# Three weight chunks loaded and split in halves at the start, first products by block over three chunks

## What is computed

```python
def rms_norm(x, g):
    xf = x.astype(jnp.float32)
    y = xf * lax.rsqrt(jnp.mean(xf * xf, axis=-1, keepdims=True) + EPS)
    return (y * g.astype(jnp.float32)).astype(x.dtype)
...
    for l in range(DEPTH):
        h = rms_norm(x, norm_mix_pre[l])
        proj = h @ w_in[l]
        qa, ka, va, qb, kb, vb = jnp.split(proj, SPLITS, axis=-1)
```

## Time and profile before

| what | value |
|---|---|
| median of 3 runs | 1076.66 us (1076.03 to 1077.01) |
| the profiled execution | 1076.21 us |
| its span | 1074.3 us |
| TensorE, matmul | 1060.6 us busy, 99% of the span |
| TensorE, weight load | 937.0 us, 87% |
| VectorE | 883.5 us, 82% |
| ScalarE | 666.4 us, 62% |
| GpSimd | 187.9 us, 17% |
| granted TensorE clock | 1.00 |

### The profile page before, as it was taken

The page is one execution under the profiler, slowest core; times in us unless marked ns, Lnnn a source line. Parts: engine busy times, 40 slices in busy tenths (PEclk is TensorE's granted clock), DMA queues, the critical chain, the costliest instruction groups (busy, mean ns, idle before and its releaser), DMA issues.

```text
span 1074.3 us, 17989 instructions
## 1 busy us (share of the span) xinstructions
PE 1060.6 (99%) x6544; PEld 937.0 (87%) x6544; DVE 883.5 (82%) x1440; ACT 666.4 (62%) x1171; POOL 187.9 (17%) x239
## 2 busy tenths in 40 slices
PE   9999999999999999999999999999999999999997
PEld 6788777998999999988888787788899999998886
DVE  6898896799988988898685788766589889879876
ACT  7887785476555555666683469645455555566664
POOL 1576754011100111000000104210011111110000
PEclk9999999999999999999999999999999999999999
DMA  7423322766776676886636720154366676777553
GB/s 297 128 60 92 86 60 75 227 129 184 203 184 205 162 184 200 192 258 205 189 133 215 171 75 1 50 157 149 97 157 167 219 169 183 204 182 224 192 178 129
DMA packets 51319, 171.16 MB, mean 159 GB/s; under 512 B 6432, under 2 KB 7072, under 8 KB 51104
## 3 DMA queue, kind: packets, MB, share of 16 engines
q1 hardware_dynamic: 37296, 122.56, 34.9%
q0 software_dynamic: 13312, 46.14, 19.8%
q10 hardware_dynamic: 624, 1.31, 0.4%
HBM read 162.64 MB, written 48.23 MB: 196 GB/s over the span
## 4 chain that ended last, share of the span: by engine, by line
PE 89%; DVE 4%; ACT 3%; POOL 2%; issue 1%; DMA 1%; SPq 0%; DVEq 0%; ACTq 0%; POOLq 0%
PE bank L2214 11%; PE bank L2213 11%; PE bank L2212 11%; PE bank L2773 7%; PE bank L2774 7%; PE bank L2775 7%; PE bank L641 6%; PE bank L642 6%; PE bank L643 6%; PE bank L1245 2%; PE bank L1235 2%; PE bank L1190 1%; PE bank L1192 1%; PE bank L1191 1%; PE bank L1334 1%
## 5 line engine op out<-in xcount | busy, mean ns | idle before, releaser
L563 DVE TENSOR_TENSOR wl<-raw,wh 128x1024 fp32r<-128x1024 f32 (+1 forms) x144 | 169.5, 1183 | 59.7 <-ACT wh L550 58.4
L550 ACT ACTIVATE wh<-raw 128x1024 fp32r<-128x1024 f32 (+1 forms) x145 | 145.8, 1010 | 110.3 <-PE bank L2775 50.0
L2212 PE MATMUL bank<-h,wh 128*128 128x256 f32 x576 | 163.0, 283 | 0.0
L2213 PE MATMUL bank<-h,wh 128*128 128x256 f32 x576 | 163.0, 283 | 0.0
L2214 PE MATMUL bank<-h,wl 128*128 128x256 f32 x576 | 163.0, 283 | 0.0
L2214 PE MATMUL bank<-hh,wl 128*128 128x256 f32 x432 | 122.3, 283 | 0.0
L2213 PE MATMUL bank<-hl,wh 128*128 128x256 f32 x432 | 122.3, 283 | 0.0
L2212 PE MATMUL bank<-hh,wh 128*128 128x256 f32 x432 | 122.2, 283 | 0.0
L2773 PE MATMUL bank<-wh,high_tokens 128*128 128x512 f32 x308 | 121.1, 393 | 0.0
L2775 PE MATMUL bank<-wh,low_tokens 128*128 128x512 f32 x308 | 120.0, 390 | 0.0
L2774 PE MATMUL bank<-wl,high_tokens 128*128 128x512 f32 x308 | 119.9, 389 | 0.0
(11 more groups left out here) (363 smaller groups left out, 2669.3 us busy)
## 6 DMA issues: line engine op xcount, KB each, us to landing
raw<-weights SPq DMA_DIRECT2D x163, 512.0 KB, 4.1
down_weight_sums<-weights POOLq DMA_DIRECT2D x60, 512.0 KB, 5.7
raw<-down_weight_sums SPq DMA_DIRECT2D x40, 512.0 KB, 4.1
down_weight_sums<-down_weight_sums POOLq DMA_DIRECT2D x20, 512.0 KB, 4.6
xres<-x_t SPq DMA_DIRECT2D x8, 512.0 KB, 6.6
down_weight_sums<-weights POOLq DMA_DIRECT2D x12, 256.0 KB, 4.4
sw<-ta SPq DMA_DIRECT2D x36, 64.0 KB, 2.0
raw<-down_weight_sums SPq DMA_DIRECT2D x8, 256.0 KB, 2.6
```

The source lines that it names most:

```text
L550: act.activation(wh[:, j, b, n], raw[:, j, b, n], ACT.Copy).then_inc(high_split, 1)
L563: v.tensor_tensor(wl[:, j, b, :], raw[:, j, b, :], wh[:, j, b, :].bitcast(F32), ALU.subtract)\
L2212: pe.matmul(o, wh_half[:, h, k, :], high[:, k, :], start=first and k == 0, stop=False, skip_group_check=True)
L2213: pe.matmul(o, wh_half[:, h, k, :], low[:, k, :], start=False, stop=False, skip_group_check=True)
```

## The change

The first three chunks are each loaded in two transfers, blocks 0 to 3 and blocks 4 to 7, and each half is split by an instruction of its own on ScalarE and on VectorE. SyncE issues half of chunk 0, x 0-1, the first halves of chunks 1 and 2, x 2-3, the three later halves, x 4-5, x 6-7, chunk 3. `START` goes by k over all three tiles instead of tile by tile; its first 18 products need k = 0 and 1 alone. The zero matmuls are 12 instead of 16. The squares of k = 0 to 3 stand behind `act_first` of k = 4 to 7, and those of k = 4 to 7 after all of them. Every later count of `high_split` and `low_split` is higher by three (`split_made`).

```diff
--- before.py
+++ after.py
@@ -93,6 +93,11 @@
 def whole(n):
 
     return n - sum(min(max(n - CHUNK0[g] - 2 * PLAIN, 0), 2 * GROUPS) for g in ("gu1", "gu2"))
+
+
+def split_made(c):
+
+    return whole(c + 1) + 3
 
 
 def group_of(c):
@@ -225,12 +230,10 @@
 assert len(SEAM1) == len(set(SEAM1)) == 12 * KT
 
 
-START = [("wh", "hh", 0, k) for k in (0, 1)] + [("wl", "hh", 0, k) for k in (0, 1)] + [("wh", "hl", 0, k) for k in (0, 1)]
-START += [("wh", "hh", 1, k) for k in (0, 1)] + [("wh", "hh", j, 2) for j in (0, 1)] + [("wl", "hh", 0, 2)]
-START += [("wl", "hh", 1, k) for k in (0, 1, 2)] + [("wh", "hl", 1, k) for k in (0, 1)]
-START += [(w, "hh", j, 3) for w in ("wh", "wl") for j in (0, 1)] + [("wh", "hl", j, k) for k in (2, 3) for j in (0, 1)]
-START += [(w, h, 2, k) for w, h in (("wh", "hh"), ("wh", "hl"), ("wl", "hh")) for k in range(4)]
-START += [(w, h, j, k) for k in (4, 5) for w, h in (("wh", "hh"), ("wl", "hh"), ("wh", "hl")) for j in range(3)]
+START = [(*HH, 0, 0), (*LH, 0, 0), (*HH, 0, 1), (*LH, 0, 1), (*HL, 0, 0), (*HH, 1, 0), (*HH, 1, 1), (*HL, 0, 1), (*HL, 1, 0), (*HL, 1, 1)]
+START += [(*HH, 2, 0), (*HH, 2, 1), (*LH, 1, 0), (*LH, 1, 1), (*HL, 2, 0), (*HL, 2, 1), (*LH, 2, 0), (*LH, 2, 1)]
+START += [(*f, j, k) for k in (2, 3, 4, 5) for f in (HH, LH, HL) for j in range(3)]
+assert len(START) == len(set(START)) == 54
 SPLIT_AT = {m: END[m] + 1 for m in END}
 SPLIT_AT.update({0: -6, 1: -2, 2: 0, 3: 2})
 SPLIT_AT.update({4: 5, 5: 12, 6: 14, 7: 21, 8: 27, 9: 35, 10: 39, 11: 47})
@@ -487,6 +490,7 @@
         x_loaded = [sem(f"x_loaded{i}") for i in range(4)]
         loaded = [sem(f"weights_loaded{i}") for i in range(RING)]
         out_stored = sem("out_stored")
+        first_loaded = [sem(f"first_halves_loaded{j}") for j in range(3)]
         high_split = sem("weights_high_split")
         low_split = sem("weights_low_split")
         used = sem("chunks_used")
@@ -549,12 +553,32 @@
             b = blocks_of(c)
             act.activation(wh[:, j, b, n], raw[:, j, b, n], ACT.Copy).then_inc(high_split, 1)
 
+        def act_first_half(act, j):
+
+            act.wait_ge(first_loaded[j], 16)
+            act.activation(wh[:, j, 0:4, :], raw[:, j, 0:4, :], ACT.Copy).then_inc(high_split, 1)
+
+        def act_later_half(act, j):
+
+            act.wait_ge(loaded[j], 16)
+            act.activation(wh[:, j, 4:8, :], raw[:, j, 4:8, :], ACT.Copy).then_inc(high_split, 1)
+
+        def vec_first_half(v, j):
+
+            v.wait_ge(high_split, j + 1)
+            v.tensor_tensor(wl[:, j, 0:4, :], raw[:, j, 0:4, :], wh[:, j, 0:4, :].bitcast(F32), ALU.subtract).then_inc(low_split, 1)
+
+        def vec_later_half(v, j):
+
+            v.wait_ge(high_split, split_made(j))
+            v.tensor_tensor(wl[:, j, 4:8, :], raw[:, j, 4:8, :], wh[:, j, 4:8, :].bitcast(F32), ALU.subtract).then_inc(low_split, 1)
+
         def vec_split(v, c):
 
             if c >= CHUNKS:
                 return
             j = c % RING
-            v.wait_ge(high_split, whole(c + 1))
+            v.wait_ge(high_split, split_made(c))
             if c == FORGET:
                 v.tensor_tensor(wh[:, j, :, LOW8], raw[:, j, :, 0:8], wh[:, j, :, 0:8].bitcast(F32), ALU.subtract)\
                     .then_inc(low_split, 1)
@@ -565,7 +589,7 @@
 
         def slot_wait(eng, c):
 
-            eng.wait_ge(low_split, whole(c + 1))
+            eng.wait_ge(low_split, split_made(c))
 
 
 
@@ -647,7 +671,7 @@
         def high_first(pe, bank, c):
 
             slot = c % RING
-            pe.wait_ge(high_split, whole(c + 1))
+            pe.wait_ge(high_split, split_made(c))
             for k in range(KT):
                 pe.matmul(bank[:, :], wh[:, slot, k, :], hh[:, k, :], start=k == 0, stop=False)
                 pe.matmul(bank[:, :], wh[:, slot, k, :], hl[:, k, :], start=False, stop=False)
@@ -1107,9 +1131,9 @@
 
             def of(self, pe, w, h, j, k):
 
-                if j >= self.made[w]:
+                if w is not None and j >= self.made[w]:
                     self.made[w] = j + 1
-                    pe.wait_ge({"wh": high_split, "wl": low_split}[w], whole(self.c0 + j + 1))
+                    pe.wait_ge({"wh": high_split, "wl": low_split}[w], split_made(self.c0 + j))
                 if k >= self.made[h]:
                     self.made[h] = k + 1
                     pe.wait_ge({"hh": self.tokens.high, "hl": self.tokens.low}[h], k + 1)
@@ -1118,12 +1142,16 @@
 
 
             pe.wait_ge(cs_zeroed, 1)
-            for _ in range(16):
+            for _ in range(12):
                 pe.matmul(banks[7][:, :], cs[:, 0:P], cs[:, :], start=True, stop=True)
             waits = Operands(0, h_in1)
+            first = {"wh": 0, "wl": 0}
             begun = set()
             for w, h, j, k in START:
-                waits.of(pe, w, h, j, k)
+                if k < 4 and j >= first[w]:
+                    first[w] = j + 1
+                    pe.wait_ge({"wh": high_split, "wl": low_split}[w], j + 1)
+                waits.of(pe, w if k >= 4 else None, h, j, k)
                 pe.matmul(bank1(j)[:, :], {"wh": wh, "wl": wl}[w][:, j, k, :], {"hh": hh, "hl": hl}[h][:, k, :],
                           start=j not in begun, stop=False)
                 begun.add(j)
@@ -3241,9 +3269,16 @@
         @block.sync
         def _(sp):
             sp.dma_start(cols[:, :], cols_in).then_inc(cols_loaded, 16)
-            for i in range(4):
-                sp.dma_start(raw[:, i, :, :], w_in[i]).then_inc(loaded[i], 16)
+            sp.dma_start(raw[:, 0, 0:4, :], w_in[0][:, 0:4, :]).then_inc(first_loaded[0], 16)
+            sp.dma_start(xres[:, 0:2, :], x_in[:, 0:2, :]).then_inc(x_loaded[0], 16)
+            for j in (1, 2):
+                sp.dma_start(raw[:, j, 0:4, :], w_in[j][:, 0:4, :]).then_inc(first_loaded[j], 16)
+            sp.dma_start(xres[:, 2:4, :], x_in[:, 2:4, :]).then_inc(x_loaded[1], 16)
+            for j in range(3):
+                sp.dma_start(raw[:, j, 4:8, :], w_in[j][:, 4:8, :]).then_inc(loaded[j], 16)
+            for i in (2, 3):
                 sp.dma_start(xres[:, 2 * i:2 * i + 2, :], x_in[:, 2 * i:2 * i + 2, :]).then_inc(x_loaded[i], 16)
+            sp.dma_start(raw[:, 3, :, :], w_in[3]).then_inc(loaded[3], 16)
             sp.dma_start(ones[:, :], mats_in[1]).then_inc(mats_loaded, 16)
             sp.dma_start(ident[:, :], mats_in[0]).then_inc(mats_loaded, 16)
             sp.dma_start(headmean[:, :], mats_in[2]).then_inc(mats_loaded, 16)
@@ -3259,7 +3294,7 @@
                     else:
                         reached(sp, fast[g].summed, len(TOKEN_SUMS) + 3 * m + 3)
                 else:
-                    sp.wait_ge(low_split, whole(c + 1 - RING))
+                    sp.wait_ge(low_split, split_made(c - RING))
                 b = blocks_of(c)
                 if down_chunk(c):
                     name, x, i = down_chunk(c)
@@ -3312,19 +3347,19 @@
             def act_first(k):
                 act.wait_ge(x_loaded[k // 2], 16)
                 act.activation(hh[:, k, :], xres[:, k, :], ACT.Copy, scale=col("mix_pre", k)).then_inc(h_in1.high, 1)
-            act_split(act, 0)
+            act_first_half(act, 0)
             act_first(0)
             act_first(1)
-            act_split(act, 1)
+            act_first_half(act, 1)
+            act_first_half(act, 2)
             act_first(2)
             act_first(3)
-            act_square(act, n_x, 0, xres[:, 0, :])
-            act_square(act, n_x, 1, xres[:, 1, :])
-            act_split(act, 2)
+            for j in range(3):
+                act_later_half(act, j)
             for k in range(4, KT):
                 act_first(k)
-                act_square(act, n_x, k - 2, xres[:, k - 2, :])
-            for k in (6, 7):
+                act_square(act, n_x, k - 4, xres[:, k - 4, :])
+            for k in range(4, KT):
                 act_square(act, n_x, k, xres[:, k, :])
             act_constants(act)
             act_split(act, 3)
@@ -3355,18 +3390,20 @@
         @block.vector
         def _(v):
             v.memset(cs[:, :].bitcast(F32), 0.0).then_inc(cs_zeroed, 1)
-            for j in (0, 1):
-                vec_split(v, j)
-                for k in (2 * j, 2 * j + 1):
-                    vec_h_low(v, k, h_in1, "mix_pre")
-            add_square(v, n_x, 0, acc)
-            add_square(v, n_x, 1, acc)
-            vec_split(v, 2)
+            vec_first_half(v, 0)
+            vec_h_low(v, 0, h_in1, "mix_pre")
+            vec_h_low(v, 1, h_in1, "mix_pre")
+            vec_first_half(v, 1)
+            vec_first_half(v, 2)
+            vec_h_low(v, 2, h_in1, "mix_pre")
+            vec_h_low(v, 3, h_in1, "mix_pre")
+            for j in range(3):
+                vec_later_half(v, j)
             for k in range(4, KT):
                 vec_h_low(v, k, h_in1, "mix_pre")
-                add_square(v, n_x, k - 2, acc)
-            add_square(v, n_x, 6, acc)
-            add_square(v, n_x, 7, acc)
+                add_square(v, n_x, k - 4, acc)
```

(2 more changed lines are left out.)

## The result

| kernel | median | lowest to highest | ratio to before (95%) |
|---|---|---|---|
| before, 11 runs beside it | 1076.48 us | 1075.62 to 1077.01 | |
| changed, 11 runs | 1078.96 us | 1077.00 to 1080.37 | 1.0023 (1.0016 to 1.0031) |

The change costs 2.5 us, where the forecast was 1076.8 and the range ended at 1078.4. The times also spread over 3.4 us, before over 1.4. The profiled execution took 1080.24 us with a span of 1078.3, the second longest of the eleven, so what its profile shows is more than the median pays.

The account below looks back on a forecast made before the run. TensorE, 99% busy, was taken as bound, with L704 awaiting the later of products (18.9) and squares (20.87). L704 moves from 20.85 to 20.87 + 0.15 = 21.02, net +0.15 on median 1076.66: 1076.8 us, range 1075.6 to 1078.4.

Parts of the forecast that it names:

- The tie of two chains at L704: Before the sum of squares on TensorE: START's products and VectorE's added squares arrive within 0.03 us of each other.
- the four signs of being wrong: L704 right behind the last product; products behind it 0.43 apart; x 4-5 past 12.2; START gaps over 0.3 us.
- chain two: Squares of x added up on VectorE: 8.27 us from low half 4 at 12.6, ready at 20.87.
- a cost that the trace bounds: First loads: three more transfers ahead of x 4-5 cost 0.0 to 0.1 us together.
- The third rival: First loads: each half costs 0.2 us beyond its bytes, x 4-5 lands 0.6 later, 1077.4 us; chance 0.06.
- The bound of 0.2 either way on this landing: First loads: x 4-5 lands at 11.8, at most 0.2 us earlier or later.
- the clock's rival: TensorE idle 2.1 us before L704 lowers the clock, costing 1.8 us: 1078.6, or 1080.4 if doubled; chance 0.11.
- Behind L704 the work moves as one block: After the sum of squares: order of work unchanged, everything from L704 on shifted by one constant.

Follow-up runs that it names:

- e6: Kernel before with only the squares and additions placed as in the change, loads and products as before: 1076.54 us, 1.0002.
- e8: Kernel before with three loads of 64 KB matrices moved from the end of the first loads to behind chunks 0, 1 and 2: 1078.08 us, 1.0017.
- e1: Changed kernel with 11 more matmuls on zeros between START's last product and the sum of squares: 1077.95 us, 1.0015.
- e5: Changed kernel with 4 matmuls on zeros between START's last product and the sum of squares: 1077.95 us, 1.0016.
- e12: e1 once more (changed kernel with 11 zero matmuls in the gap), on the same chip as e11: 1077.90 us, 1.0016.
- e11: Changed kernel run once more without further edit, on the same chip as e12: 1078.94 us, 1.0022.
- e2: Kernel before with chunks 0 to 2 each loaded in two transfers, blocks 0 to 3 and 4 to 7, behind each other: 1077.43 us, 1.0010.
- e3: Kernel before with chunks 0 to 2 each loaded in two transfers of 64 partitions, rows of full length: 1079.09 us, 1.0032.
- e10: Kernel before with chunk 0 alone in halves, its later half loaded behind x 2-3, and 12 warm-ups: 1076.63 us, 1.0004.
- e7: Changed kernel with squares 0 and 1 in ScalarE's idle stretches, additions 0 to 3 on GpSimd, three products ahead of the sum of squares: 1078.38 us, 1.0018.

## Why the prediction was wrong

**The frame held.** The tie of two chains at L704, and that the edit speeds up the products alone, is what the profile after shows: START ends at 19.36 (forecast 18.9; its first 18 products take 4.65 us from 6.55 to 11.20, where 4.1 and a wait of 0.15 were counted), then TensorE stands and waits. Of the four signs of being wrong that the prediction names, two came: x 4-5 past 12.2, and products 0.43 apart behind L704. The sum of chain two from low half 4 on was 8.27 and measured 8.21 here and 8.12 in e6.

**The step that failed first is "a cost that the trace bounds".** I took 0.0 to 0.1 us for three more transfers, from a row where four small ones and a large one land within 3.4 us behind x 6-7. That was a row of another kind. What it gives is a time from one landing to a later one; it didn't price a transfer ahead of the one that is waited for. Three of the same small transfers, put there in e8, cost x 4-5 2.1 us. In the changed kernel's profile x 4-5 lands 1.25 later than forecast, and the sum of squares with it: 22.00 instead of 20.87. In the seven other profiles with these loads it lands 0.4 to 1.2 later. The third rival had this mechanism, and its size (0.6 us) is near the middle of the eight; its chance of 0.06 was far too low. The bound of 0.2 either way on this landing was too narrow as well, since two profiles with the same loads can differ by 0.8 us. The Trainium skill (DMA: Bandwidth & Descriptors, Anatomy of one DMA), which I set aside because 6 us was plainly too much, had the right sign; the delay of x 4-5 in the trace lies between the two. This step alone would have left the time within the range: e1, e5 and e12, which have the late loads and keep the clock in their profiles, are at 1077.90 to 1077.95.

**The second step is the chance of the clock's rival.** It was given 0.11 and came true; it is what took the time out of the range. Its price, 1.8 us, was nearly right (1.6 in the profiles of the changed kernel and e11, 1.0 in the medians). I forecast a gap of 2.1 us and had no row with more than 1.0; between these I should have put far more than one in ten. The runs now show clock 1.00 behind idle stretches of 1.16 and 1.55 us and also behind e8's 2.33, and 0.50 behind 1.87, 2.06 and 2.62. That is no threshold, and the two groups in the changed kernel's times say that the same gap costs in some executions only. The Trainium skill (TensorE: Matmul & The Clock Gate, Part 1) says that the moment of such a transition varies from run to run; the spread agrees with that. Both failures lean on each other: a later sum made the gap longer.

**The balance.** With the gap filled, e12 is 1077.90 - 1076.23 = 1.67 us over before. In its profile the squares are added up 0.8 later (21.50 instead of 20.70), the last zero matmul holds L728 up for another 0.5, and 0.3 us come at the end of the program. From a mark in the second block (the first tile of its gate and up projection) to the last product the changed kernel takes 1072.01 - 762.80 = 309.2, before 1068.07 - 759.17 = 308.9; in the changed kernel a split on ScalarE waits 0.59 us there instead of 0.30. All eight profiles with the changed loads have these 309.2, and before, e2, e3, e6, e8 and e10, which were made from the kernel before, have the 308.9; what causes it was not traced. The clock adds 1.0 in the median, and somewhat more if the filling's own 0.5 is counted, for e12 pays that and e11 doesn't. So the changed kernel's 2.5 and e11's 2.7 are the late squares (0.6 to 1.3 by the profiles), these 0.3, and for the rest the clock.

**"Behind L704 the work moves as one block"** held to within 0.5 us: in the profiled executions the delay is 2.86 at the heads' sum, 3.31 at 213 us, and 3.94 at the last product. Of what comes between these marks, 0.3 is the wait at the end that was just named, and part is a later landing of the swapped halves near 33 us (4.3 us at most instead of 3.6); part stays open. In e11 the delay is 2.20 at the heads' sum, 2.27 at 213 us and 3.16 at the last product.

## What to carry to other kernels

Where two chains end at the same instruction within 0.1 us, speeding up one of them earns only idleness, and on TensorE idleness of about 2 us cost another 1.6 in some half of the executions through the clock. Splitting loads to start earlier let the first x land 0.6 sooner (5.65 instead of 6.25 in the changed kernel) and x 4-5 0.4 to 1.25 later, so ask which later load stands on the other chain before splitting. If a gap can't be avoided, a few useless matmuls in it (four here) bring back what the clock would take; more than the gap holds delay what stands behind it. And a landing read from one profile has a spread: look at a second profile before a bound of 0.2 us is put on it.

## What the runs showed of the hardware

One to three more transfers among the first loads, at DMA engines shown as busy almost all the time (share 0.94 to 1.02), brought 395 and 398 GB/s down to between 342 and 356. Transfers over 64 of 128 partitions brought it down to 280 (one profile).

An idle stretch of TensorE of 1.87 us was enough for the granted clock to go to 0.50, and one of 2.33 us in another place left it at 1.00. In the three profiles with a fall the clock stood at 0.50 for some 3.4 us (changed kernel: from 22.0 to 25.4). In e11 it fell about 1 us after TensorE had gone back to work, so the gap itself doesn't show it.

GpSimd's additions, 1.6 us each, slowed VectorE's instructions with two inputs beside them from 0.67 to 1.7 us from start to start. The Trainium skill (GPSIMD Engine Reference, the specification table's row on SBUF interfaces) names just this, contention with VectorE's instructions that have two inputs in SBUF; e7 agrees with it.
